# Expert results added to two sums in memory by DMA, in place of rows of their own that are summed at the end

## What is computed

```python
scores = sigmoid(xt @ w_router)                    # 512 x 64, 8 chosen per token
step:  xb = xt[tok]                                # up to 128 tokens of one expert
       hb = silu(xb @ w_gate[e]) * (xb @ w_up[e])
       yb = (hb @ w_down[e]) * g[:, None]          # g: the token's weight for this expert
       acc = acc.at[tok].add(yb)
out = rms_norm(h + gate2 * (acc + shared), norm_f_g)
```

## Time and profile before

| | |
|---|---|
| median of 3 runs | 1357.01 us (1354.59 to 1357.18) |
| the profiled execution | 1351.99 us, its span 1350.2 us |
| TensorE's granted clock, mean | 0.949 of 2.4 GHz; 1.00 from 700 to 1280 us |
| PE busy | 1191.1 us, 88% of the span |
| DVE, ACT, POOL busy | 576.9, 231.8, 266.1 us |
| moved by DMA | 318.35 MB; read from memory 303.71, written 31.46 MB |
| last DMA of the last expert pass issued | 1286.08 us |

### The profile page before, as it was taken

The page is one execution under the profiler, slowest core; times in us unless marked ns, Lnnn a source line. Parts: engine busy times, 40 slices in busy tenths (PEclk is TensorE's granted clock), DMA queues, the critical chain, the costliest instruction groups (busy, mean ns, idle before and its releaser), DMA issues. The chain is left out here.

```text
span 1350.2 us, 12868 instructions
## 1 busy us (share of the span) xinstructions
PE 1191.1 (88%) x4460; PEld 585.5 (43%) x4461; DVE 576.9 (43%) x1201; ACT 231.8 (17%) x458; POOL 266.1 (20%) x254
## 2 busy tenths in 40 slices
PE   0799677788999999989789999999999999999954
PEld 0544455444555444435344444444444444444421
DVE  5336899797642403424722222222222222222238
ACT  3412221132334000120011111111111111111111
POOL 7861478100000000020111111111111111111100
PEclk9799787898899999989889999999999999999978
DMA  8635000430404123022789999999999999999276
GB/s 330 172 110 194 9 10 9 164 153 3 187 1 156 63 93 109 32 71 117 295 346 390 371 398 399 400 371 382 398 393 367 378 396 393 360 359 388 82 307 272
DMA packets 85765, 318.35 MB, mean 236 GB/s; under 512 B 30706, under 2 KB 33778, under 8 KB 57026
## 3 DMA queue, kind: packets, MB, share of 16 engines
q1 hardware_dynamic: 64084, 277.96, 53.2%
q0 software_dynamic: 15216, 36.24, 7.1%
q10 hardware_dynamic: 6400, 3.33, 1.1%
HBM read 303.71 MB, written 31.46 MB: 248 GB/s over the span
## 5 line engine op out<-in xcount | busy, mean ns | idle before, releaser
L1506 PE MATMUL ps<-uTs,ring 128*128 128x512 f32 (+2 forms) x496 | 228.2, 618 | 3.7 <-DMA ring<-in_w_in 3.0
L1774 PE MATMUL ps<-ring,XT 128*128 128x512 f32 x512 | 225.1, 592 | 0.4 <-ACT XT L981 0.4
L1368 DVE TENSOR_TENSOR uTs<-uTs,ps 128x256 f32<-128x256 f32 x50 | 21.1, 421 | 300.2 <-ACT uTs L985 300.2
L1506 PEld LDWEIGHTS ps<-uTs,ring 128*128 128x128 f32 (+2 forms) x496 | 95.5, 196 | 123.1 <-issue 118.2
L1774 PEld LDWEIGHTS ps<-ring,XT 128*128 128x128 f32 x512 | 95.1, 191 | 107.7 <-issue 107.1
L721 POOL DMA_INDIRECT XT<-u_rows,idx x51 | 52.0, 1020 | 433.7 <-DVE idx L1357 424.6
L1802 PE MATMUL ps<-ring,XT 128*64 128x512 f32 x576 | 127.6, 595 | 0.9 <-ACT XT L981 0.9
L1813 PE MATMUL ps<-ring,uTs 128*128 128x512 f32 x256 | 119.4, 610 | 0.1
L1409 DVE TENSOR_SCALAR uTs<-ps,gat 128x512 f32<-128x512 f32 x50 | 37.5, 751 | 125.4 <-PE ps L1813 78.9
L1486 PEld LDWEIGHTS ps<-ident,XT 128*128 128x128 f32 x448 | 55.9, 188 | 57.4 <-DMA XT<-u_rows,idx 43.0
L1486 PE MATMUL ps<-ident,XT 128*128 128x128 f32 x448 | 63.8, 287 | 18.5 <-DMA XT<-u_rows,idx 12.4
(11 more groups left out here) (320 smaller groups left out, 1381.0 us busy)
## 6 DMA issues: line engine op xcount, KB each, us to landing
ring<-in_w_exp_gate SPq DMA_DIRECT2D x64, 1024.0 KB, 7.8
ring<-in_w_exp_up SPq DMA_DIRECT2D x64, 1024.0 KB, 12.5
ring<-in_w_exp_down SPq DMA_DIRECT2D x64, 1024.0 KB, 11.5
ring<-in_w_ada SPq DMA_DIRECT2D x12, 2048.0 KB, 12.2
ring<-in_w_in SPq DMA_DIRECT2D x7, 2048.0 KB, 9.4
ring<-expert_rows SPq DMA_DIRECT2D x6, 2048.0 KB, 18.6
ring<-in_w_out SPq DMA_DIRECT2D x2, 2048.0 KB, 8.8
H<-in_x SPq DMA_DIRECT2D x1, 2048.0 KB, 14.2
```

The lines of the kernel that those rows point to most:

```text
L1506: ins = mm(b[0:rows_, 0:cols], l, r, start=(k == 0), stop=(k == len(chunks) - 1))
L1774: ins = mm(a3(ps[0][:, :], 2), xgT[par][:, k], wgu[r][:, k], start=(k == 0), stop=(k == KD - 1))
```

## The change

There are two sums in memory, `expert_sum0` and `expert_sum1`, of 512 rows of 1024 each. SyncE fills them with zeros early on, from `W3`. In the passes GpSimd adds the rows of `ye` to the token's row of one of them by an indirect DMA with an addition. A pass with one expert adds to one sum, by the parity of its load. A pair may hold a token in both halves, so it makes two DMAs, one to each sum; `off_half` puts the other half's indices out of bounds. Two additions to one sum must not overlap, so GpSimd waits before each for the one before it to that sum. At the end SyncE reads 4 MB in 8 DMAs of 0.5 MB, GpSimd adds the two sums of a tile, and VectorE goes on from there. The place column of `RG`, its scan and `part_place` are gone, and so are TensorE's products at the end. The list of places of each slot, `adx`, is now made in `result`.

```diff
-RC = 6
+RC = 5
+ADDS, _n = [], [0, 0]
+for _p, _units in enumerate(PASSES):
+    _to = (0, 1) if len(_units) == 2 else (LOAD_OF[_units[0][0]] % 2,)
+    for _a in _to:
+        _n[_a] += 1
+    ADDS.append([(_a, _n[_a]) for _a in _to])
...
-    YD = nc.dram_tensor("expert_rows", (SEQ * EK, DM), F32, kind="Internal").ap()
+    ACC = [nc.dram_tensor(f"expert_sum{n}", (SEQ, DM), F32, kind="Internal").ap() for n in range(2)]
...
         def added(eng, p):
             if p >= 0:
-                eng.wait_ge(y_added[p % 2], 16 * (p // 2 + 1))
+                for to, n in ADDS[p]:
+                    eng.wait_ge(y_added[to], 16 * n)
...
                 if g == ("misc", 0):
                     state_tables()
+                    sp.wait_ge(S["zeros"], 1)
+                    for j in range(TT):
+                        for n in range(2):
+                            sp.dma_start(ACC[n][P * j:P * (j + 1), :], W3).then_inc(S["acc_zero"], 16)
...
-            for n in range(2 * TT):
-                sp.dma_start(y_part[n], token_rows[n // 2][:, HALF_ROW * (n % 2):HALF_ROW * (n % 2 + 1)]).then_inc(rows_in[n], 16)
+            for t in range(TT):
+                sp.dma_start(XT[:, DM * t:DM * (t + 1)], ACC[0][P * t:P * (t + 1), :]).then_inc(sum_in[t], 16)
+                sp.dma_start(ut4[:, t], ACC[1][P * t:P * (t + 1), :]).then_inc(sum_in[t], 16)
...
-            def scatter(y, col, s):
+            def add(to, y, col, s):
                 pool.sem_inc(S["pool_turn"], 1)
-                E.indirect_dma_start(YD, bass.IndirectOffsetOnAxis(adx[:, col:col + 1], 0), y, None,
-                                     bounds_check=SEQ * EK - 1, oob_is_err=False).then_inc(s, 16)
+                E.indirect_dma_start(ACC[to], bass.IndirectOffsetOnAxis(adx[:, col:col + 1], 0), y, None,
+                                     compute_op=ALU.add, bounds_check=SEQ - 1, oob_is_err=False).then_inc(s, 16)
...
-            def scatter_pass(p):
+            pool.wait_ge(S["acc_zero"], 32 * TT)
+            def add_pass(p):
                 pool.wait_ge(S["y_out_s"], p + 1)
                 pool.wait_ge(S["y_out_v"], p + 1)
-                scatter(ye[p % 2], p % AC, y_added[p % 2])
+                for h, (to, n) in enumerate(ADDS[p]):
+                    if n > 1:
+                        pool.wait_ge(y_added[to], 16 * (n - 1))
+                    add(to, ye[p % 2], 2 * (p % 2) + h, y_added[to])
...
             pool.sem_inc(S["all_added"], 1)
+            for t in range(TT):
+                pool.wait_ge(sum_in[t], 32)
+                E.tensor_tensor(ut4[:, t], ut4[:, t], XT[:, DM * t:DM * (t + 1)], ALU.add).then_inc(S["sums_joined"], 1)
...
-            V.tensor_scalar(tok8, tokt, float(EK), 8.0 * EK + 1.0, ALU.mult, ALU.add)
+            for h, side in enumerate((sg, nsg)):
+                link(V.tensor_scalar(off_half[:, h:h + 1], side, -float(SEQ), float(SEQ), ALU.mult, ALU.add))
...
-            V.tensor_tensor_scan(scr[:, 512:768], scr[:, 256:512], scr[:, 768:1024], 0.0, ALU.mult, ALU.add).then_inc(S["place_ok"], 1)
...
-            dve.wait_ge(S["place_ok"], 1)
-            link(V.tensor_tensor(wk, wk, bc(tok8, NE, 2), ALU.subtract))
-            link(V.tensor_tensor(RG[:, :, 0:NE, 2], wk, Mm, ALU.mult))
...
             def take_list(col, s, count, L=ps[5]):
-                V.tensor_copy(part_place[col % 2], L[:, 2:3])
...
-                if to is not None:
-                    dve.wait_ge(s[1], count)
-                    row_of_sum(to, col)
...
             def result(p):
                 dve.wait_ge(S["expert_done"], p + 1)
                 added(dve, p - 2)
+                row = idx[:, p % RING:p % RING + 1]
+                for h in range(len(PASSES[p])):
+                    ax = adx[:, 2 * (p % 2) + h:2 * (p % 2) + h + 1]
+                    if len(PASSES[p]) == 1:
+                        V.tensor_copy(ax, row)
+                    else:
+                        V.tensor_scalar(ax, row, off_half[:, h:h + 1], None, ALU.add)
...
                 if t < TT:
-                    dve.wait_ge(rows_in[2 * t + 1], 16)
-                    y = y_part[2 * t + 1]
-                    link(V.tensor_tensor(y[:, 0:2 * DM], y[:, 0:2 * DM], y[:, 2 * DM:4 * DM], ALU.add))
-                    x = y[:, 0:DM]
-                    link(V.tensor_tensor(x, x, y[:, DM:2 * DM], ALU.add))
-                    dve.wait_ge(S["sums_ok"], t + 1)
-                    for n in range(2):
-                        c = slice(512 * n, 512 * (n + 1))
-                        ins = V.tensor_tensor(x[:, c], x[:, c], ps[2 * (t % 2) + n][:, :], ALU.add)
-                    signal(ins, "sums_taken", t + 1)
+                    dve.wait_ge(S["sums_joined"], t + 1)
+                    x = ut4[:, t]
                     link(V.tensor_tensor(x, x, ADA[:, 5 * DM:6 * DM], ALU.mult))
...
-            for t in range(TT):
-                if t >= 2:
-                    pe.wait_ge(S["sums_taken"], t - 1)
-                pe.wait_ge(rows_in[2 * t], 16)
-                for n in range(2):
-                    for k in range(EK // 2):
-                        ins = mm(ps[2 * (t % 2) + n][:, :], ident[:], y_part[2 * t][:, DM * k + 512 * n:DM * k + 512 * (n + 1)],
-                                 start=(k == 0), stop=(k == EK // 2 - 1))
-                ins.then_inc(S["sums_ok"], 1)
```

More of the change, by code:

```diff
@@ L261, in build @@
         for n in """x_in c_in b_in norm_in lam_in ct_in bt_in dt_in dsk_in bglu_in bias_in consts ada_zero
-                c_silu dt_exp angles sines squares u_tile ada_sum pool_turn u_perm inverse root empties ov_em b_ok ba_ok ca_ok w2_ok phase_args phases zeros place_ok sums_ok sums_taken scan_zero g1_in rstd_ok modulation u_ok_v u_ok_s gates_ok toeplitz
+                c_silu dt_exp angles sines squares u_tile ada_sum pool_turn u_perm inverse root empties ov_em b_ok ba_ok ca_ok w2_ok phase_args phases zeros acc_zero scan_zero g1_in rstd_ok modulation u_ok_v u_ok_s gates_ok toeplitz
                 u_rows u_chunks rotated relu_free causal dist t_max prob av_done y_att y2_ok mixed h_out
@@ L267, in build @@
                 y_out_s y_out_v ov_list ov_out ov_row ov_go ov_hot ov_ldone ov_idx ov_x ov_xt ov_xs ov_xv ov_gu
-                ov_silu ov_h ov_ht ov_hts ov_y ov_yo ov_add all_added fin_add fin_sq final out_done""".split():
+                ov_silu ov_h ov_ht ov_hts ov_y ov_yo ov_add all_added sums_joined fin_add fin_sq final out_done""".split():
             S[n] = ctx.enter_context(nc.semaphore(n))
@@ L273, in build @@
         b_in = [ctx.enter_context(nc.semaphore(f"b_in{n}")) for n in range(2)]
-        rows_in = [ctx.enter_context(nc.semaphore(f"rows_in{n}")) for n in range(2 * TT)]
+        sum_in = [ctx.enter_context(nc.semaphore(f"sum_in{t}")) for t in range(TT)]
         s_in = [ctx.enter_context(nc.semaphore(f"stream_in{s}")) for s in range(3)]
@@ L337, in build @@
         idx = sb("idx", [P, RING + 2], I32)
-        AC = 2 * RING
-        adx = sb("adx", [P, AC + 2], I32)
+        adx = sb("adx", [P, 4], I32)
         gat = sb("gat", [P, RING + 2])
-        tok8 = sm[:, 284:288]
+        off_half = sm[:, 284:286]
         ids = kT[0:1, 256:256 + NE].bitcast(I32)
         part_row = [sm[:, 280 + n:281 + n] for n in range(2)]
-        part_place = [sm[:, 288 + n:289 + n] for n in range(2)]
         RGs = UB[:, 0:TT * NEP * RC // 2].bitcast(BF16)
@@ L755, in _ @@
                 if p:
-                    scatter_pass(p - 1)
+                    add_pass(p - 1)
             pool.wait_ge(S["ov_idx"], 1)
             gather(0, OC, S["ov_x"])
-            scatter_pass(NP - 1)
+            add_pass(NP - 1)
             added(pool, NP - 2)
@@ L777, in _ @@
                                 pool.wait_ge(S["ov_yo"], j * 2 + 4)
-                                scatter(ye[u], AC + u, S["ov_add"])
+                                add(u, ye[u], 2 * u, S["ov_add"])
                                 pool.wait_ge(S["ov_add"], j * 16 + 16)
@@ L857, in s5_apply @@
                 if q == 0:
-                    act.wait_ge(S["zeros"], 1)
+                    act.wait_ge(S["acc_zero"], 32 * TT)
                 for j in range(CH):
@@ L1345, in hot_pass, with take_list @@
                 ins.then_inc(S["slot_hot"], 1)
-            def row_of_sum(to, col):
-                V.scalar_tensor_tensor(adx[:, to:to + 1], idx[:, col:col + 1], float(EK), part_place[col % 2], ALU.mult, ALU.add)
-            def take_list(col, to, s, count, L=ps[5]):
+            def take_list(col, s, count, L=ps[5]):
                 r = part_row[col % 2]
-                V.reduce_sum(gat[:, col:col + 1], L[:, 3:RC], axis=AX.X)
-                V.tensor_copy(part_place[col % 2], L[:, 2:3])
+                V.reduce_sum(gat[:, col:col + 1], L[:, 2:RC], axis=AX.X)
                 V.tensor_scalar(r, L[:, 1:2], 8.0 * P, None, ALU.add).then_inc(s[0], 1)
@@ L1378, in _ @@
                 dve.wait_ge(S["list_done"], p + 1)
-                take_list(p, p, em_s, p + 1, ps[6])
```

(3 more changed lines are left out.)

22 lines of the change are left out of this document (9 added, 13 removed).

## The result

The changed kernel takes **1366.25 us**, the median of 5 runs (1362.57 to 1367.12), beside 1356.75 of the kernel before on the same chip (5 runs, 1353.91 to 1357.18). The ratio is 1.0070, with a 95% interval of 1.0056 to 1.0083: 9.5 us slower, with 27 predicted (1384). Its profiled execution took 1366.55 us, of which 1364.8 are span, so it lies at the median of its kernel. That of the kernel before lay 5 us under the median of its own.

A forecast was written before the change was run, and what follows sets the result against it. It took TensorE as the nearer limit in the expert stage, the DMA engines also near theirs, and the end as a separate chain. -26.1 - 2.1 + 53 + 2.8 = +27.6 us on the median 1357.0 gave 1384, range 1335 to 1430.

The forecast's parts named there:

- Step 4: Expert stage: the adds bring 88 us of DMA work, 35 of it hidden, so the stage grows by 53 us.
- The price of an add: Expert stage: an add costs the DMA engines three transfers where the write cost one, a transfer being 44 us for all rows.
- What hides it: Expert stage: 20 us of added DMA work fit in the engines' idle rest, about 15 in the weights' lead.
- rival B: Expert stage: the add's second read streams, so an add costs two transfers; -17.7 us, 1339; chance 0.28.
- The signs: Profile: software queue's share up from 7.1% to about 13%, DMA share 1.0 throughout the passes; about 10% would show B.
- The last sign of the prediction: Passes: if they grow while the DMA engines are not full, the cost is a wait and not the engines' work.
- D: Passes: adds beyond four transfers hold up the next gather; at five +118 us, 1475; chance 0.14.
- 1 us a pass: Passes: TensorE waits, for weights or for gathers, 1 us in each pass.
- Step 1: The end: smaller reads, GpSimd's sums mostly hidden behind VectorE, 5.2 us a further tile; 26.1 us less.
- Step 2: Before the expert stage: VectorE loses the scan, two lines and two small copies, gains one small operation; 2.1 us less.
- Step 3: Early on: writing 4 MB of zeros ahead of ada piece 4 is hidden, 0; uncovered it would cost 14 us.
- Step 5: After the last pass: the last add is not hidden, two more transfers and the index column; 2.8 us more.

The follow-up runs named there:

- e8_late_before: The kernel before, with an order of passes in which the last pairs come later; 1356.25 us, ratio 0.9986.
- e1_plain: The changed kernel with every add made a plain write of the same rows, so its output is not the layer's; 1330.03 us, ratio 0.979.
- e3_twice: The kernel before with every row written twice, the second time to another tensor, nothing added; 1388.35 us, ratio 1.0229.
- e2_half: The changed kernel with adds to the first sum only and plain writes to the second, so not the layer's output; 1349.45 us, ratio 0.9944.
- e6_less: The changed kernel with plain writes for adds and the writes to the second sum left out, so not the layer's output; 1326.60 us, ratio 0.977.
- e4_end_pe: The changed kernel with the two sums of a tile added at the end by TensorE in place of GpSimd; 1363.67 us, ratio 1.0062.
- e10_fill_short: The changed kernel with 19.2 us of unread TensorE products ahead of the waits for weights in six paired passes; 1367.76 us, ratio 1.0090.
- e11_fill_end: e10_fill_short with TensorE adding the two sums at the end as in e4_end_pe, against the changed kernel; 1366.60 us, ratio 1.0078.

## Why the prediction was right and wrong, step by step

The direction was right, by a balance of the same two large terms, a shorter end against a longer stage, but the size was 18 us too high. Of these 18, 13.0 are of the sum (27.6 predicted, 14.6 between the profiles), and 4.8 come from carrying the 5 us between profile and median over to the changed kernel, whose profile lay at its median. That the direction came out is in part luck: the price of an add was set too high, and what would hide its work too high as well. With the right price alone the same sum gives 1339, faster than before.

**Step 4, the expert stage: +53 predicted, +34 measured** (32.9 up to the fiftieth gather, and from there to the last issue 36.1 us in place of 35.0). Two parts of this step failed, with opposite signs. The 34 may hold up to 3.5 us of luck: e8_late_before, whose work is that of the kernel before and whose profile lies at its median, takes 612.1 us from the third gather to the last write, where the profile of the kernel before has 608.6. Against e1_plain's 610.0 the growth is 32.6.

*The price of an add.* I took three transfers, because a write cannot begin before its operands have met. The software queue's engines' time is 97.0 us in e1_plain and 141.9 with adds: 44.9 for what I had called one transfer of 44, so an add costs two, 2.02 times the write (2.08 with the price of a write from e3_twice). e2_half gives the same by its half (9.1% of 1347.9 is 122.7, +25.7). The rule of the Trainium skill (Collectives: The Full Stack, "The bandwidth ceiling: the fold count and why AG ≠ RS ≠ AR") that I had weighed and set aside, stated there for a ring of ranks, is that the second source read halves the rate; these runs, of one core, agree with it.

*What hides it.* I let 20 us vanish in the idle rest of the DMA engines and 15 in the weights' lead at the end. At the right price that leaves 9, and rival B, built on the same two numbers, said 1339. The measured growth is almost four times that. The idle rest was not filled in any run: the DMA share from the third to the fiftieth gather is 0.96 or 0.97 in the kernels before and after and in e1, e2 and e3, and only e6_less, with less to do than today, reads 0.95. The windows behind a wait show the likely reason. A pair takes two loads at once out of a ring of four; when they have been late, the engines catch up, the ring is full, and they fall to 0.59 until a slot is free (0.55 from 986 to 989, behind the wait of 2.96 us at the pair of 980.20). Of the lead a little is there: from the fiftieth gather to the last add, 36.1 us, they read a share of 0.35 where they read 0.23, 4.6 us.

What counts is the sum of both large queues. Engines' time is the share times the span. A share is rounded to 0.1%, which is 0.7 us for each entry and up to 2.7 for a difference of two sums:

| kernel | q0 | q1 | sum, against e1_plain | span, against e1_plain |
|---|---|---|---|---|
| e6_less | 79.4 | 702.8 | -13.8 | -5.4 |
| e1_plain | 97.0 | 699.0 | 0 | 0 |
| e2_half | 122.7 | 692.8 | +19.5 | +19.0 |
| changed kernel | 141.9 | 690.6 | +36.5 | +35.9 |

From e1_plain up, the span grows by what the engines' time grows by, 1 to 1. Below, 13.8 us of work less took 5.4 off the span, and only 2.3 of these off the stage. The packets of q1 take less of the engines' time the more the software queue has to do (702.8, 699.0, 692.8, 690.6 us down the table), and that is no matter of the addition: with every row written twice, e3_twice, they take 707.1 us where the kernel before has 718.3. So nothing shows the weights' packets held up by a shortage of memory bandwidth; why they take less is not settled, no run here takes a packet apart. e3_twice fits less closely: +30.2 of both queues against the kernel before, +36.3 of span. Its last write, too, is doubled behind the last pass.

*The signs.* The software queue took 10.4%, not the 13% forecast but the 10% of rival B; the DMA share stayed at 0.96 where 1.0 was forecast. The last sign of the prediction, that growth with DMA engines not full would mean a wait and not their work, would have misled: the passes grew at a share of 0.96, and e1_plain and e3_twice show that the engines' work did it.

*The form was as predicted:* TensorE waits for weights; D, gathers held up behind adds, is excluded (waits for gathered rows fell from 12.4 to 6.8 us), and so are GpSimd's waits for the earlier add, 2.6 and 5.7 us in all. "1 us a pass" was wrong as a picture: they come in ten places, up to 5.1 us.

**Step 1, the end: -26.1 predicted, -20.9 measured.** The reading was right: GpSimd's first sum began 4.94 us after the first read's issue, 4.7 by the working, and each further tile takes 5.1 us (1348.95 to 1354.06), 5.2 predicted. I had let GpSimd's sums lie beside VectorE "even at twice their price" without asking what they do to VectorE. Three operations lost 2.0 us each: 3.25 to 3.27 us is just the 3.23 us of a GpSimd sum beside them. The Trainium skill (SBUF — State Buffer, "🔬 SBUF: two separate sides") says that a VectorE operation with two inputs in SBUF and a GpSimd operation that reads SBUF share a port pair as a lock, held for the whole instruction. The rows agree that each holds up the other, though taking strict turns would make 2.34 + 1.24 = 3.58 us a round (an estimate), and 3.2 to 3.3 was measured; and e4_end_pe, which takes the sums off GpSimd, has 1.24 us again. By that rule the term could have been foreseen. It is 6 us; the rest is within 1.

**Step 2, before the stage: -2.1 predicted.** The third gather came 1.5 us earlier (677.48 to 675.96), but this difference of two traces is smaller than the spread: over the ten kernels that carry the change it comes at 674.9 to 680.3. The term itself shows in GpSimd's idle time from its last fill of a tile to the first gather, in which VectorE builds the tables: 46.5 us in the kernel before (46.50, and 46.57 and 46.49 in e3 and e8), 43.7 to 43.8 in all ten with the change. So 2.7 us were gained, 2.1 predicted. The index column earlier in the pass is worth nothing that can be seen.

**Step 3, the zeros: 0.** The eight DMAs landed in a median of 6.1 us. They moved SyncE's issue of ada piece 4 from 53.27 to 65.05, and VectorE still takes it at 85.04 (85.22 before): hidden there, as forecast. GpSimd's fill ahead of the stage begins at 601.1, 601.4 and 602.3 us in the three kernels without the zeros and at 600.8 to 605.1, a mean of 602.9, in the ten with them; whether they cost a microsecond on the way isn't shown.

**Step 5, the last add: +2.8 predicted, +3.1 measured** (9.26 us from the last add's issue to the first read, 6.20 before). It was priced at two transfers more where one was right; 0.6 us of the difference is the longer issue (1.58 for 0.99), and the rest no run takes apart.

Together: -1.5 + 32.9 + 1.1 + 3.1 - 20.9 = +14.7, with 14.6 between the spans. The gain at the end would have been used up, by my reckoning, at 2.4 transfers per add; in truth two were enough, since nearly nothing of them was hidden.

No kernel tried here computes the layer and is faster than the kernel before by more than can be told. One was not tried: a mixture in which some of a token's results are written to rows of their own and the others added. e2_half, in which the written results don't pile up and so need no further reading at the end, is at 0.9944 [0.9922, 0.9966], and a true mixture would have, by estimate, 7.6 us (1357.08 less 1349.45) for the rows that it reads back and sums besides.

## What to carry to other kernels

Where a DMA's share reads 0.97 and the consumer is 98% busy, price a further transfer at its full time and do not count on the missing 3%: here no run filled them, and where they were looked at they were gaps behind a late pair, in which the ring of buffers was full. Test the bend from both sides before such a change (here: every write twice, and half of the writes left out), because the same microsecond of DMA work cost one on the one side and at most 0.4 on the other (5.4 of 13.8 us; in the stage itself 2.3). And a slowed operation that a trace shows is not yet a cost: put work in its place, and see whether the end moves.

## What the runs showed of the hardware

- An indirect DMA that adds to memory took the engines 2.02 to 2.08 times the time of the same write, and GpSimd 1.58 us to issue in place of 1.01; alone, 128 rows of 4 KB landed in 6.3 us from the issue in place of 3.3.
- In the changed kernel, after waits of 2.9 to 5.1 us in front of a product TensorE's granted clock read 0.50 to 0.71 over the product's first 3 us (it took 8.8 to 9.6 us in place of 7.09), and 1.00 where extra products filled them. After waits of 0.8 to 1.7 us the product took 7.1. In e10_fill_short one took 9.95 after 3.75. The length of the wait alone does not decide: in e11_fill_end two products took 7.09 after waits of 3.25.
- Operations on two tiles of 128x1024 on GpSimd and VectorE at once took 3.2 us on each, against 2.34 and 1.24 alone: VectorE goes at GpSimd's pace.
- A sum through TensorE at the end was slower for the first tile than GpSimd's (5.2 us against 2.35), at a clock granted at 0.51 from 1332 to 1335 us; at 1.00 a tile takes TensorE 3.4 us.
